# Weight splits four chunks ahead, one in front of each epilogue and one inside it, in a two-block transformer kernel

## The reference, cut to what matters

```
u = hn @ w_ffn_in                       # 1024 -> 2 * 2816
c = conv_b + sum(conv_w[j] * up[:, j:j + l] for j in range(3))
gate, val = split(c, 2)
out = (silu(gate) * val) @ w_ffn_out    # 2816 -> 1024
```

## Time and profile before

| | |
|---|---|
| median of 3 runs | 3484.1 us (3483.82 to 3484.87) |
| the profiled execution's own time | 3486.14 us |
| its span, first to last instruction | 3484.3 us |
| instructions | 54701 |
| PE busy | 3150.8 us (90% of the span) |
| DVE busy | 1779.3 us (51%) |
| ACT busy | 1423.1 us (41%) |
| POOL busy | 371.5 us (11%) |
| mean granted TensorE clock | 0.914 of 2.4 GHz |
| chain that ended last, by engine | PE 77%, DVE 9%, ACT 6%, issue 5% |

### The profile page before, as it was taken

The page is one execution under the profiler, slowest core; times in us unless marked ns, Lnnn a source line. Parts: engine busy times, 40 slices in busy tenths (PEclk is TensorE's granted clock), DMA queues, the critical chain, the costliest instruction groups (busy, mean ns, idle before and its releaser), DMA issues.

```text
span 3484.3 us, 54701 instructions
## 1 busy us (share of the span) xinstructions
PE 3150.8 (90%) x20792; PEld 2780.1 (80%) x20792; DVE 1779.3 (51%) x2514; ACT 1423.1 (41%) x1980; POOL 371.5 (11%) x330
## 2 busy tenths in 40 slices
PE   4999998998999988997799898888998998988888
PEld 2667665647999988997698895788986988948888
DVE  2223224365555566554457457556554573574664
ACT  1222113135445444444443435644444434365443
POOL 2001000052101101110002101010100020010110
PEclk7999999989999999998897697899998966978999
DMA  7985456502655644654253051244542511503443
GB/s 246 285 251 157 131 171 163 163 1 81 185 182 145 184 142 144 188 183 133 73 169 92 23 172 48 97 121 142 167 151 75 174 54 55 175 13 122 123 142 127
DMA packets 586147, 474.64 MB, mean 136 GB/s; under 512 B 28721, under 2 KB 547889, under 8 KB 585665
## 3 DMA queue, kind: packets, MB, share of 16 engines
q1 hardware_dynamic: 584464, 460.44, 43.3%
q0 software_dynamic: 1520, 11.95, 1.1%
HBM read 471.23 MB, written 4.72 MB: 137 GB/s over the span
## 4 chain that ended last, share of the span: by engine, by line
PE 77%; DVE 9%; ACT 6%; issue 5%; SPq 1%; DMA 1%; DVEq 0%; ACTq 0%; POOL 0%
PE PS L1578 21%; PE PS L1579 20%; PE PS L1580 20%; PE PS L964 3%; PE PS L1507 3%; DVE CB L1970 2%; ACT high L1639 2%; PE PS L501 1%; PE PS L1280 1%; PE PS L1289 1%; DVE low L1786 1%; SPq L1445 1%; PE PS L806 1%; PE PS L794 1%; PE PS L1015 1%
## 5 line engine op out<-in xcount | busy, mean ns | idle before, releaser
L1786 DVE TENSOR_TENSOR low<-raw,high 128x1024 fp32r<-128x1024 f32 (+1 forms) x744 | 902.8, 1228 | 996.2 <-ACT high L1639 993.1
L1639 ACT CAST high<-raw 128x1024 fp32r<-128x1024 f32 (+1 forms) x744 | 762.9, 1034 | 992.2 <-PE PS L1580 722.4
L1578 PE MATMUL PS<-NHh,high 128*128 128x272 f32 x2496 | 743.2, 298 | 109.4 <-DVE low L1786 35.3
L1580 PE MATMUL PS<-NHh,low 128*128 128x272 f32 x2496 | 732.6, 294 | 0.0
L1579 PE MATMUL PS<-NHl,high 128*128 128x272 f32 x2496 | 730.6, 293 | 0.0
L1578 PE MATMUL PS<-XH,high 128*128 128x256 f32 (+1 forms) x1856 | 589.5, 318 | 52.1 <-DVE XL L1828 31.1
L1578 PEld LDWEIGHTS PS<-NHh,high 128*128 128x128 f32 x2496 | 481.8, 193 | 130.4 <-DVE low L1786 43.2
L1579 PE MATMUL PS<-XL,high 128*128 128x256 f32 (+1 forms) x1856 | 582.3, 314 | 0.0
L1580 PE MATMUL PS<-XH,low 128*128 128x256 f32 (+1 forms) x1856 | 581.8, 313 | 0.0
L1579 PEld LDWEIGHTS PS<-NHl,high 128*128 128x128 f32 x2496 | 482.5, 193 | 0.0
L1580 PEld LDWEIGHTS PS<-NHh,low 128*128 128x128 f32 x2496 | 481.3, 193 | 0.0
(11 more groups left out here) (280 smaller groups left out, 4116.5 us busy)
## 6 DMA issues: line engine op xcount, KB each, us to landing
raw<-w_in_dram SPq DMA_DIRECT2D x416, 256.0 KB, 3.0
raw<-ffn_w_in_dram SPq DMA_DIRECT2D x352, 256.0 KB, 3.7
part<-ada_w_dram SPq DMA_DIRECT2D x184, 256.0 KB, 4.1
raw<-w_ffn_in_dram SPq DMA_DIRECT2D x176, 256.0 KB, 3.4
raw<-ffn_w_out_dram SPq DMA_DIRECT2D x160, 256.0 KB, 3.2
raw<-w_branch_dram SPq DMA_DIRECT2D x96, 256.0 KB, 2.9
raw<-w_ffn_out_dram SPq DMA_DIRECT2D x80, 256.0 KB, 3.1
part_sg<-ada_w_dram SPq DMA_DIRECT2D x48, 256.0 KB, 3.0
```

What stands on the lines that cost most here:

```text
L1578: nc.tensor.matmul(out, wh, xh, start=(k0 + k == 0), stop=False)
L1580: last = nc.tensor.matmul(out, wl, xh, start=False, stop=(c == len(kch) - 1 and k == nk - 1))
L1639: nc.scalar.copy(high[:, slot, 0:nk, :], raw[:, slot, 0:nk, :]).then_inc(s_high, 1)
L1786: nc.vector.tensor_tensor(low[:, slot, 0:nk, :], raw[:, slot, 0:nk, :], high[:, slot, 0:nk, :].bitcast(F32), ALU.subtract).then_inc(s_low, 1)
```

## The change

`ahead` now yields the chunk `NSLOT` (4) ahead instead of 3, in the slot of the chunk that it replaces. `behind` puts all of a unit's splits but the last in front of the epilogue, the last one right behind `epilogue`, and then calls a new function `second` with what used to be the end of the epilogue: on ACT the casts GH of glu and bgate, the sigmoid of conv and the squares of add; on DVE the two products of conv. The cast G2H of conv leaves its epilogue for `conv_high`, called at the head of the next unit's epilogue (and once behind the last). In the prologue chunks 0 and 1 are split first, and chunks 2 and 3 behind the first split of the activations (ACT) and behind the first modulation (DVE).

```diff
--- before.py
+++ after.py
@@ -423,21 +423,28 @@
 
             nch = len(s["kch"])
             for c in range(nch):
-                S = s["S0"] + 2 * nch * i + nch * p + c + 3
-                if not isinstance(S, int) or S < n_chunks:
-                    yield S, slot_of(s, p, c + 3), s["kch"][c + 3][1] if c + 3 < nch else 4
-
-        def behind(eng, s, split, epilogue, between=None, after=None):
+                S = s["S0"] + 2 * nch * i + nch * p + c + NSLOT
+                nk = s["kch"][c + NSLOT][1] if c + NSLOT < nch else 4
+                yield S, slot_of(s, p, c), nk, not isinstance(S, int) or S < n_chunks
+
+        def behind(eng, s, split, epilogue, second=None, between=None, after=None):
 
             def two(i, first=False):
                 for p in range(2):
-                    for Q, slot, nk in ahead(s, i, p):
-                        split(Q, slot, nk)
+                    u = 2 * i + p
+                    *early, (S_last, slot_last, nk_last, more) = ahead(s, i, p)
+                    for S, slot, nk, wanted in early:
+                        if wanted:
+                            split(S, slot, nk)
                     if first and not p and between:
                         between()
-                    epilogue(2 * i + p, p)
+                    epilogue(u, p)
+                    if more:
+                        split(S_last, slot_last, nk_last)
+                    if second:
+                        second(u, p)
                     if after:
-                        after(2 * i + p)
+                        after(u)
 
             two(0, True)
             if rolled(s):
@@ -1656,9 +1663,11 @@
             act.wait_ge(s_tokens, 16)
             cin = cols[:, COLS["c"]:COLS["c"] + 2 * KT]
             nc.scalar.activation(scf[:, 0:2 * KT], cin, ACT.Sigmoid).then_inc(s_silu, 1)
-            for S in range(3):
+            for S in range(2):
                 split_high(S, S, 4)
             split_x_high(0)
+            for S in range(2, NSLOT):
+                split_high(S, S, 4)
             for s in steps:
                 name, T = s["name"], s["T"]
 
@@ -1671,16 +1680,10 @@
                         act.wait_ge(s_chunk, done)
                         nc.scalar.activation(SG[:, p:p + 1, 0:T], bank(p, 0)[:, :, 0:T],
                                              ACT.Sigmoid).then_inc(s_act, 1)
-                        act.wait_ge(s_free, U + 3)
-                        nc.scalar.copy(GH[:, bass.ds(u, 1), 0:T], SG[:, p:p + 1, 0:T]).then_inc(s_hh, 1)
                     elif name == "cgate":
                         act.wait_ge(s_chunk, done)
                         act.wait_ge(s_free, U + 1)
                         nc.scalar.copy(SG[:, p:p + 1, 0:T], bank(p, 0)[:, :, 0:T]).then_inc(s_act, 1)
-                    elif name == "bgate":
-                        act.wait_ge(s_free, U + 3)
-                        nc.scalar.copy(GH[:, bass.ds(2 * u, 2), 0:T],
-                                       SG[:, p, :].rearrange("p (a t) -> p a t", a=2)).then_inc(s_hh, 1)
                     elif name in ("gate", "mgate"):
                         act.wait_ge(s_chunk, done)
                         nc.scalar.activation(gate_room(s, 2 * u), bank(p, 0, 2)[:, :, 0:T],
@@ -1692,6 +1695,8 @@
                         nc.scalar.activation(MI[:, bass.ds(16 + 2 * u, 2), :], ps, ACT.Sigmoid,
                                              scale=-1.0).then_inc(s_act, 1)
                     elif name == "conv":
+                        if not isinstance(u, int) or u:
+                            conv_high(u - 1, 1 - p)
                         act.wait_ge(s_chunk, done)
                         for j in range(2):
                             ft = FT * j + u
@@ -1699,11 +1704,25 @@
                                                  bias=col("conv_b", s["layer"] * 2 * FT + ft),
                                                  scale=col("conv_w", (3 * s["layer"] + 2) * 2 * FT + ft)
                                                  ).then_inc(s_act, 1)
+
+                def conv_high(u, p):
+                    act.wait_ge(s_gb, s["gb0"] + u + 1)
+                    nc.scalar.copy(G2H[:, bass.ds(u, 1), :], SG2[:, 2 + p:3 + p, :]).then_inc(s_hh, 1)
+
+                def second(u, p):
+                    U = s["U0"] + u
+
+                    if name == "glu":
+                        act.wait_ge(s_free, U + 3)
+                        nc.scalar.copy(GH[:, bass.ds(u, 1), 0:T], SG[:, p:p + 1, 0:T]).then_inc(s_hh, 1)
+                    elif name == "bgate":
+                        act.wait_ge(s_free, U + 3)
+                        nc.scalar.copy(GH[:, bass.ds(2 * u, 2), 0:T],
+                                       SG[:, p, :].rearrange("p (a t) -> p a t", a=2)).then_inc(s_hh, 1)
+                    elif name == "conv":
                         act.wait_ge(s_free, U + 3)
                         nc.scalar.activation(SG2[:, p:p + 1, :], CB[:, 2 * p:2 * p + 1, :],
                                              ACT.Sigmoid).then_inc(s_act, 1)
-                        act.wait_ge(s_gb, s["gb0"] + u + 1)
-                        nc.scalar.copy(G2H[:, bass.ds(u, 1), :], SG2[:, 2 + p:3 + p, :]).then_inc(s_hh, 1)
                     elif name == "add":
                         rms_act_pair(act, rmss, u, s["U0"] + 4)
 
@@ -1721,7 +1740,9 @@
                     def between():
                         hg_logs(act, s["layer"])
 
-                behind(act, s, split_high, epilogue, between)
+                behind(act, s, split_high, epilogue, second, between)
+                if name == "conv":
+                    conv_high(FT - 1, (FT - 1) % 2)
                 if name == "gate" and s["tile"] == 32:
                     level_exps(act, s["layer"], 0)
                 if s.get("norm"):
@@ -1877,6 +1898,8 @@
             columns(0)
             dve.wait_ge(s_tokens, 48)
             modulate(0, X, T1)
+            for S in range(2, NSLOT):
+                split_low(S, S, 4)
             for s in steps:
                 name, T = s["name"], s["T"]
                 if name == "cgate":
@@ -1996,7 +2022,7 @@
                         hg_cumulate(dve, link, s["layer"])
                         right_exponents(dve, s["layer"], 0)
 
-                behind(dve, s, split_low, epilogue, between,
+                behind(dve, s, split_low, epilogue, second, between,
                        (lambda u: ada_turns(s["U0"] + u)) if s["S0"] <= HOST[-1] else None)
                 if s is steps[0]:
                     dve.wait_ge(s_mod, 2)
```

## The result

The changed kernel took 3420.4 us (median; 3414.8 to 3424.5), the kernel before beside it 3484.5: a ratio of 0.9816, 95% interval 0.9802 to 0.9831, or 64 us less. With five later runs of the same kernel the median of nine is 3418.7. The forecast was 3423 (3409 to 3441).

A forecast was written before the change was run, and what follows sets the result against it. TensorE, busy 90% of the span, was taken as the bound, starved in convolution by an ACT-DVE loop. Span 3484.3 - 58.0 (convolution) - 13.9 (prologue) + 10.8 (step ends) = 3423.2 us; median forecast 3423, range 3409 to 3441.

The forecast's parts named there:

- The conv loop: Two convolution steps: splits no longer wait for sigmoid, products and G2H, so TensorE's rate holds; 58.0 us gained.
- The collision: Convolution: POOL's G2L would now run beside DVE's low split, costing DVE up to 0.56 us a unit, within the room.
- Rows 7: Profile rows cited for convolution: a low split beside 0.56 us of POOL work took 1.64 us, a free one 1.23 or less.
- rival of a DVE bound: Convolution: DVE becomes the bound at about 6.4 us a unit; 3434 to 3440 us, chance 0.11.
- The start: Prologue: DVE's copy no longer stands behind chunk 2, so the first product comes earlier; 13.9 us gained.
- rival of loads: Prologue: weight loads hold the beginning, so its 13.9 us isn't gained; 3437 us, chance 0.07.
- The ends: Ends of steps: the next step's fourth chunk is split ahead of work behind the last epilogue; 10.8 us lost.
- Differential attention: Beginning of that step: L875 releases TensorE but must wait for high and low split; 1.6 us twice, 3.2 lost.
- Y: Cast of Y: it can't run ahead of the last chunk any more, DVE moves by a split; 2.4 us lost.
- recurrence: Recurrence: the exponentials' table load follows ACT's last sigmoid at once and is delayed; 1.05 us twice, 2.1 lost.
- attention: Attention: the long TB addition follows DVE's last copy at once and is on the path; 1.2 us lost.
- Slower: Convolution: the split inside the epilogue waits for its raw load, holding sigmoid, products and banks; 3494 us, chance 0.02.

The follow-up runs named there:

- old_conv: Changed kernel with both convolution edits undone (fourth split behind the unit's sigmoid work, product tile cast in its own unit): 3473.5 us.
- after: The changed kernel itself, whole change in place, against the kernel before: 3420.4 us in its first four runs, 3418.7 the median of nine.
- cast_kept: Changed kernel with one convolution edit undone: ACT casts the product tile in its own unit again, the split inside the epilogue stays: 3445.7 us.
- split_behind: Changed kernel with one convolution edit undone: the fourth split follows the unit's sigmoid work again, the cast stays one unit later: 3417.7 us.
- start_only: Kernel before with only the prologue order changed: two chunks split ahead of x, the third behind it, on both engines: 3470.5 us.
- four_ahead: Changed kernel with prologue and convolution both as before, leaving splits four chunks ahead in all other steps: 3486.9 us, ratio 1.0009.
- old_start: Changed kernel with the prologue order of before: three chunks split ahead of x, the fourth behind it, on both engines: 3428.2 us.

## Why the prediction was right, and where it wasn't

- **The conv loop: right.** 58.0 forecast; matched products give 28.1 and 29.0 us for the two steps with the addition behind each, 57.1, and old_conv 54.8 to 59.1. The first step fell from 160.8 to 135.5 us where 133.8 was forecast, since more than its first products ran at half clock (mean 0.98 over the step); the addition behind gave 2.8 instead of 2.0.
- **Which edit does it: wrong by omission.** The prediction gave the gain to the split that no longer waits for sigmoid, products and G2H, and never asked what the cast moved alone would do. By the runs the cast alone brings all of it, and the split alone half. With the cast gone ACT makes both splits right behind the sigmoid, DVE waits 0.50 us for the sigmoid in a unit and not for a split, and that order fits into TensorE's unit as well. The sum needed only that the loop opens, and so hid the mistake.
- **The collision: the row was misread.** "By the row it loses 0.56 us": DVE lost nothing. Rows 7 show a DVE instruction that starts while POOL's is under way; in conv POOL comes second. In after 42 of the 44 G2L start within a low split and end 0.63 us behind it; the low splits that they meet keep their 1.22. The prediction didn't think of the same collision in glu and bgate, where the cast GH now stands behind the split: GL (256 columns) takes 1.16 us there instead of 0.74. TensorE waits 0.8 us for a GL once in the whole kernel, so that cost nothing to speak of. The Trainium skill's rule (SBUF — State Buffer, "SBUF: two separate sides"), that a two-input DVE instruction and a GpSimd one exclude each other for whole instructions, gave this outcome, and the trace agrees: 1.02 to 1.23 us in after, 0.77 in cast_kept, where no low split is near. That G2L also waits out the second of two low splits that follow each other (1.57 us in split_behind) is what the trace adds. DVE is busy 40.9 to 41.3 us in 50, 5.0 a unit, so neither this nor the rival of a DVE bound had any weight.
- **The start: right.** 13.9 forecast, 13.6 measured alone (start_only), with the copy at 39.34 for "39.7". The load of chunk 2 was there when ACT came to it; that of chunk 3 arrived 0.76 us after ACT was ready and cost nothing, since DVE was still at the activations, so the rival of loads falls.
- **The ends: the waits right, the sum wrong.** Differential attention 2.9 for 3.2, Y 2.2 for 2.4, recurrence 1.8 for 2.1, attention 1.1 for 1.2 (the longest wait for ROT, 3.3 us instead of 2.2). But with start and conv as before the splits cost 2.8 us and not 10.8. The step that failed is the addition itself: each delay was taken to cost its length, with the granted clock behind it unchanged. In four_ahead four stretches shrank by 11 us together, three behind unchanged waits and the recurrence behind a longer one (3.4 us instead of 2.4), and in all four the granted clock was higher. That this is what the sum lacked is shown by one profile of each kernel; why the clock holds there with the splits moved stays open. Where the two ends were held, the waits gave 5.4 us and the time at least 9.
- **A small term was missed.** In the first glu step TensorE waits 1.0 us for a part of `ada_w`; that stretch is 1.3 us longer than before, 1.6 in four_ahead. In old_start that wait is absent, and a later wait of before for such a part, 1.4 us, is absent in after, so what it costs on balance isn't known. That the ring now takes loads in another order there is argued, not tried.
- That 3423 lay within 3 us of 3420 is in part luck. With the ends at 2.8 the sum is 3415, which is where the repetition lies (3414.4); the first four runs happened to be longer.
- A slip without weight: under "Slower" four chunks at the pace of before are put at 15.1 us; twice 7.49 is 15.0.

## What to carry to other kernels

When two engines wait for each other in a loop, look for the one instruction that closes it and move that behind the next unit's work: here moving one cast of 0.42 us was worth 56 us (old_conv less split_behind), and the split that was moved with it added nothing. Splits made further ahead land on the ends of steps, where nobody needs them early; holding back the two that TensorE waits behind made the fastest version. A sum of delays was good for the waits here, but in the stages full of short waits the clock behind them moved the time by as much as the waits did; an edit worth 10 us or less in such stages has to be measured.

## What the runs showed of the hardware

- The same products behind the same waits ran at the full or at half the clock in two runs of one kernel (24 products: 4.25 or 7.00 us), and with several such places the times of a kernel scatter: of the nine runs of after the four shortest (3413.6 to 3414.8) have a mean clock of 0.917 to 0.920, the four longest (3421.4 to 3424.5) 0.914 to 0.916. The changed kernel's nine runs spread over 10.9 us; the kernel before spread over 1.2 in the first four and over 10.5 in the fifteen of the last comparison (3479.8 to 3490.4), so it isn't the change that does it. Why a place goes one way or the other wasn't settled.
- When a POOL instruction and a DVE instruction with two SBUF inputs meet, the later one waits: POOL's 0.77 us became 1.02 to 1.23 behind what was left of one low split and about 1.56 with a second one behind it, while the splits kept their 1.22; and DVE's 1.23 became 1.64 behind POOL. The later one then needs a little less than its whole time: 0.63 us of 0.77 behind the split, 1.08 of 1.23 behind POOL.
